# Blank products around the spreading of the first norm's weights and behind the first transposes, in a two-layer encoder trunk

## The reference

```python
def rmsnorm(x, g):
    xf = x.astype(jnp.float32)
    y = xf * lax.rsqrt(jnp.mean(xf * xf, axis=-1, keepdims=True) + EPS)
    return (y * g.astype(jnp.float32)).astype(x.dtype)

for l in range(DEPTH):                    # DEPTH = 2
    hn = rmsnorm(h, mix_pre[l])           # l = 0: the first norm, weights mix_pre[0]
    mix = rglru_mixer(hn, ...) if l == 0 else swa_sink_attention(hn, ...)
    h = h + rmsnorm(mix, mix_post[l])
    f = swiglu(rmsnorm(h, ffn_pre[l]), ffn_w_gu[l], ffn_w_down[l])
    h = h + rmsnorm(f, ffn_post[l])
```

## Time and profile before

| | us |
|---|---|
| median of 3 runs | 1109.94 (1109.6 to 1110.15) |
| the profiled execution | 1110.47 |
| its span | 1108.7 |
| TensorE products busy | 1095.7 (99% of the span) |
| TensorE weight loads busy | 980.3 (88%) |
| VectorE busy | 782.2 (71%) |
| ScalarE busy | 557.0 (50%) |
| GpSimd busy | 14.9 (1%) |

### The profile page before, as it was taken

One profiled execution on the slowest core, in us unless ns is written; L12 is line 12 of the kernel. 1 busy time (PEld: TensorE's weight loads), 2 busy tenths in 40 slices (PEclk: granted clock), 3 DMA queues, 4 the chain that ended last, 5 costly groups with the idle time before them and its releaser, 6 DMA issues.

```text
span 1108.7 us, 17385 instructions
## 1 busy us (share of the span) xinstructions
PE 1095.7 (99%) x6901; PEld 980.3 (88%) x6901; DVE 782.2 (71%) x1117; ACT 557.0 (50%) x980; POOL 14.9 (1%) x34
## 2 busy tenths in 40 slices
PE   8999999999999999999999999999999999999998
PEld 7887787889899999988888888889899999998886
DVE  5878985788688888853357888558788888863334
ACT  5377474565355555532235576555355555542223
POOL 1000000000000000000020000000000000000000
PEclk9999999999999999999999989999999999999999
DMA  6332233234133333332242132141233333343211
GB/s 203 95 106 68 77 106 114 95 98 129 41 115 115 102 90 115 134 115 95 99 118 50 39 95 58 39 114 49 86 115 114 98 94 115 115 133 99 101 48 76
DMA packets 150961, 107.22 MB, mean 97 GB/s; under 512 B 23921, under 2 KB 140769, under 8 KB 150882
## 3 DMA queue, kind: packets, MB, share of 16 engines
q1 hardware_dynamic: 150882, 106.12, 31.8%
HBM read 104.01 MB, written 2.10 MB: 96 GB/s over the span
## 4 chain that ended last, share of the span: by engine, by line
PE 97%; ACT 1%; DVE 1%; DMA 0%; issue 0%; DVEq 0%; SPq 0%
PE ps L1787 11%; PE ps L1789 11%; PE ps L1791 11%; PE ps L1565 10%; PE ps L1566 10%; PE ps L1569 10%; PE ps L1545 9%; PE ps L1547 9%; PE ps L1546 9%; PE ps L1718 1%; PE ps L1891 1%; PE ps L1575 1%; PE ps L1918 1%; PE ps L1945 1%; PE ps L1943 1%; PE ps L1941 1%
## 5 line engine op out<-in xcount | busy, mean ns | idle before, releaser
L1005 DVE TENSOR_TENSOR w_lo<-raw,w_hi 128x1024 fp32r<-128x1024 f32 x107 | 133.1, 1247 | 166.6 <-ACT w_hi L586 166.4
L586 ACT CAST w_hi<-raw 128x1024 fp32r<-128x1024 f32 x108 | 112.6, 1046 | 168.6 <-PE ps L1569 147.5
L1787 PE MATMUL ps<-t_hi,w_hi 128*128 128x256 f32 x576 | 163.2, 283 | 0.2
L1789 PE MATMUL ps<-t_lo,w_hi 128*128 128x256 f32 x576 | 163.0, 283 | 0.0
L1791 PE MATMUL ps<-t_hi,w_lo 128*128 128x256 f32 x576 | 163.0, 283 | 0.0
L1545 PE MATMUL ps<-x_hi,w_hi 128*128 128x512 f32 (+1 forms) x424 | 154.3, 364 | 0.6 <-DVE x_lo L1035 0.6
L1546 PE MATMUL ps<-x_lo,w_hi 128*128 128x512 f32 (+1 forms) x424 | 151.6, 358 | 0.0
L1547 PE MATMUL ps<-x_hi,w_lo 128*128 128x512 f32 (+1 forms) x424 | 151.5, 357 | 0.0
L1565 PE MATMUL ps<-w_hi,t_hi 128*128 128x512 f32 x352 | 137.2, 390 | 0.0
L1566 PE MATMUL ps<-w_lo,t_hi 128*128 128x512 f32 x352 | 137.0, 389 | 0.0
L1791 PE MATMUL ps<-x_hi,w_lo 128*128 128x256 f32 x432 | 122.3, 283 | 0.0
(11 more groups left out here) (218 smaller groups left out, 2160.4 us busy)
## 6 DMA issues: line engine op xcount, KB each, us to landing
raw<-in_ffn_w_gu SPq DMA_DIRECT2D x88, 512.0 KB, 4.4
raw<-in_ffn_w_down SPq DMA_DIRECT2D x44, 512.0 KB, 3.3
raw<-in_a_w_in SPq DMA_DIRECT2D x24, 512.0 KB, 3.9
raw<-in_a_w_out SPq DMA_DIRECT2D x12, 512.0 KB, 3.3
raw<-in_b_w_q SPq DMA_DIRECT2D x16, 256.0 KB, 3.3
raw<-in_b_w_o SPq DMA_DIRECT2D x16, 256.0 KB, 3.8
h<-in_x SPq DMA_DIRECT2D x4, 512.0 KB, 5.5
result<-h SPq DMA_DIRECT2D x3, 512.0 KB, 2.6
```

What stands on the lines that cost most here:

```text
L586: nc.scalar.copy(halves(t)[0], raw[:, t % 4, :]).then_inc(w_hi_ready, 1)
L1005: v.tensor_tensor(lo, raw[:, t % 4, :], hi.bitcast(F32), ALU.subtract).then_inc(w_lo_ready, 1)
L1787: nc.tensor.matmul(ps[:, b, 0:HS], w_hi[:, slot, cols], hi, start=start, stop=False, skip_group_check=True)
L1789: nc.tensor.matmul(ps[:, b, 0:HS], w_hi[:, slot, cols], lo, start=False, stop=False, skip_group_check=True)
```

## The change

- A tile `blank` of 128 x 512 in bf16 is laid where `y_hi` will be later. VectorE fills it with zeros as its first instruction and counts `blank_ready`.
- TensorE first waits for it and then runs three products of 128 x 128 with 128 x 512 of it into bank 5, whose result is not used (`busy`). Then it waits for the identity and the norm weights as before.
- The spreading is cut into four pieces of 256 columns, with a blank product behind each. `gain_spread` is counted once for each half, and VectorE waits for the first half before its first part and for the second before its second.
- A blank product follows each of the first four groups of four transposes.
- TensorE takes `first_half(1)` ahead of `first_turn(4)`. ScalarE casts tile 1 ahead of the square of block 2, and tile 2 ahead of the high part of block 2. VectorE takes the low part of tile 1 ahead of the normalising of block 2, and that of tile 2 ahead of the low part of block 2.

```diff
--- before.py
+++ after.py
@@ -195,6 +195,7 @@
     dist_i = sb("dist_i", [P, WIN], I32, at["e_u"] + 4 * P)
     dist_n = sb("dist_n", [P, WIN], F32, at["e_u"] + 8 * P)
     gain_row = sb("gain_row", [1, D], F32, at["y_lo"])
+    blank = sb("blank", [P, S], BF16, at["y_hi"])
 
 
     at["top"] = U
@@ -307,6 +308,7 @@
         xhi_ready = sem("xhi_ready")
         xlo_ready = sem("xlo_ready")
         eps_ready = sem("eps_ready")
+        blank_ready = sem("blank_ready")
         xf_ready = sem("xf_ready")
         t_ready = sem("t_ready")
         thi_ready = sem("thi_ready")
@@ -616,11 +618,11 @@
             split_hi(0)
             for i in range(4):
                 first_high(i)
+            split_hi(1)
             square_x(2)
-            split_hi(1)
             square_x(3)
+            split_hi(2)
             first_high(4)
-            split_hi(2)
             first_high(5)
             act.wait_ge(lam_abs, 1)
             nc.scalar.activation(sp_t[:, 1, :], sp_t[:, 0, :], ACT.Exp, scale=-1.0).then_inc(lam_exp, 1)
@@ -1020,8 +1022,8 @@
                 t, k0, k1 = START_PARTS[i]
                 n = pre_at(-1, t)
                 r = reciprocal(n) if k0 == 0 else rstd[:, n:n + 1]
-                if i == 0:
-                    dve.wait_ge(gain_spread, 1)
+                if i < 2:
+                    dve.wait_ge(gain_spread, i + 1)
                 if t >= 2:
                     dve.wait_ge(first_turned, 2 * t - 2)
                 cols = slice(k0 * P, k1 * P)
@@ -1035,15 +1037,16 @@
                 v.tensor_tensor(x_lo[:, k0:k1, tok], turned_in(t)[:, k0:k1, :], x_hi[:, k0:k1, tok].bitcast(F32),
                                 ALU.subtract).then_inc(first_lo, 1)
 
+            v.memset(blank[:, :], 0.0).then_inc(blank_ready, 1)
             for i in range(4):
                 normalise_x(i)
             for i in range(4):
                 first_low(i)
+            split_lo(1)
             normalise_x(4)
-            split_lo(1)
             normalise_x(5)
+            split_lo(2)
             first_low(4)
-            split_lo(2)
             first_low(5)
 
 
@@ -1658,12 +1661,23 @@
                     token_half(b, 2, t, 1)
 
 
+            def busy(n):
+
+                for _ in range(n):
+                    nc.tensor.matmul(bank(5), blank[:, 0:P], blank[:, :], start=True, stop=True)
+
+            pe.wait_ge(blank_ready, 1)
+            busy(3)
             pe.wait_ge(ident_ready, 1)
             pe.wait_ge(gain_landed, 16)
             for half in range(2):
-                ins = nc.tensor.matmul(bank(6 + half), ones_row[:, :], gain_row[:, half * S:half * S + S], start=True,
-                                       stop=True)
-            ins.then_inc(gain_spread, 1)
+                for part in range(2):
+                    cols = slice(half * S + part * HS, half * S + part * HS + HS)
+                    ins = nc.tensor.matmul(ps[:, 6 + half, part * HS:part * HS + HS], ones_row[:, :], gain_row[:, cols],
+                                           start=True, stop=True, skip_group_check=True)
+                    if part == 1:
+                        ins.then_inc(gain_spread, 1)
+                    busy(1)
 
             def first_turn(i):
                 t, k0, k1 = START_PARTS[i]
@@ -1680,9 +1694,10 @@
 
             for i in range(4):
                 first_turn(i)
+                busy(1)
             first_half(0)
+            first_half(1)
             first_turn(4)
-            first_half(1)
             first_turn(5)
             first_half(2)
             pe.wait_ge(params_landed, 16 * 8)
```

## The result

| | before | changed |
|---|---|---|
| median of 20 runs | 1109.73 (1106.67 to 1111.52) | 1110.53 (1109.83 to 1113.47) |
| profiled execution, its span | 1110.47, 1108.7 | 1110.2, 1108.4 |

The ratio of the two is 1.0017, 95% interval 1.001 to 1.0024: the changed kernel is slower by 1.1 to 2.7 us. The forecast was 2.6 us less. The profiled execution of before was one of its long ones, so the two traces have nearly the same span although the kernels differ.

What follows compares the result with a forecast made beforehand. TensorE, busy 99%, was taken as the bound. 2.3 us from the pace, 0.2 from the start and 0.1 from the switch made 2.6 less than 1109.94: 1107.3 us, range 1105.4 to 1111.0.

Steps and rivals of the forecast that it cites:

- if the one-row passes count with the blanks: Start of TensorE's queue: one-row spreading passes and blanks together raise the clock, so transposes and first tile run fast; 2.3 us.
- The rise: Doubling of TensorE's pace, forecast at 5.5 to 6.4 us, after unbroken work from 1.15; in the earlier trace at 16.9.
- Before 11.70 to 16.95: First tile's 24 projection products, taken as slow before; forecast 11.5 to 14.4, gain with the start 2.55 us.
- the slower rival: TensorE's start: blanks don't raise the clock, first product at 12.7, 1.0 late; time 1110.4, chance 0.17.
- Blank, piece, blank: Spreading: 256-column pieces cost the same 3.4 us in all, a blank 0.43 slow; second normalising waits about 0.1 us.
- The one of the late rise: TensorE's start: pace doubles only during transposes, at 12.8, first product near 12.6; gain 1.3, time 1108.6, chance 0.13.
- The later fall of the clock: Attention part, 634.72 to 644.96: a rival said this slow stretch goes away, worth 4.7 us; time 1102.6, chance 0.12.
- the memset: VectorE's filling of the blank tile at the start: ready between 0.8 and 1.4, taken as 1.1, cost nothing.
- the spreading's start: TensorE after the three first blanks: spreading begins some 0.2 us late (0 to 0.6) against 2.23.
- the fast tile once the clock is up: First tile: 24 products 0.12 us apart, 2.9 us instead of 5.25.
- the order without a hole: Tile 1 right behind tile 0: no TensorE wait appears, though two places have only 0.15 to 0.75 us of room.
- the gain from one switch less: Transposes of block 2 moved next to block 3's save one switch between the two kinds, about 0.1 us.

Runs made afterwards that it cites:

- e11: e1 with the spreading done three times over, 10.57 us of one-row passes; one profiled execution, not timed, rise at 21.64.
- e12: Changed kernel with the spreading's pieces multiplying 128 rows (ones by zeros with the weights in the first row); one profiled execution, 1112.9 us.
- e4: As e3, but the spreading multiplies 128 rows, zeros except the weights in the first; ratio to before 1.0000 (0.9991 to 1.0008).
- e1: Kernel before with only the new order of the engines' steps, no blanks, spreading uncut; ratio to before 0.9999 (0.9991 to 1.0007).
- e2: Changed kernel with every blank product left out, spreading still in four pieces, new order kept; ratio to before 1.0004 (0.9994 to 1.0014).
- e3: Changed kernel with the spreading uncut, one-row, and three blanks behind it; ratio to before 0.9998 (0.9988 to 1.0008).
- e5: Changed kernel with blanks only where TensorE idles: three behind the uncut spreading, one behind the fourth transpose group; ratio to before 0.9992 (0.9983 to 1.0002).
- e6: Changed kernel without the four blanks behind the transposes; ratio to before 1.0019 (1.0008 to 1.0031).
- e7: Changed kernel once more, no edit; ten executions, ratio to before 1.0017 (1.0008 to 1.0027), shortest span 1107.8.
- e8: Kernel before once more, no edit; one profiled execution, span 1106.6.
- e9: Kernel before with 15 tiny one-row products behind the spreading and the blank tile's memset; ratio to before 1.0006 (0.9994 to 1.0018).
- e10: e5 repeated to narrow its interval; ratio to before 0.9990 (0.9981 to 0.9998).

## Why the prediction was wrong

**The step that failed: "if the one-row passes count with the blanks".** It was marked as the assumption of the forecast, and it carried 2.3 of the 2.6 us. The rise was forecast for 5.5 to 6.4 and came at 12.02 and 13.86. e11 refutes the assumption alone; e12 (9.49) and e4 (8.10) show the early rise with 128 rows in its place, though with a spreading that starts 1.5 us later. Only one row and 128 were tried, nothing between. What the clock did follow in all fourteen traces is full-array work: the rise came 3.2 to 5.4 us after the start of an unbroken stretch of it, in the changed kernel 3.2 and 5.1 us after the start of the spreading's last blank. (Start and rise: before 11.70, 16.90; changed 8.79, 12.02; e1 7.45, 10.78; e2 12.47, 16.53; e3 6.29, 11.46; e4 4.12, 8.10; e5 6.04, 9.99; e6 8.78, 13.29; e7 8.78, 13.86; e8 7.35, 11.38; e9 7.37, 11.65; e10 6.16, 10.27; e11 18.11, 21.64; e12 4.12, 9.49.) Not every stretch brought it: the transposes of 3.7 us in before's first trace, e2 and e11 did not. The row that could have warned me was in the earlier trace rows and I used it only for a rival: 3.75 us of one-row passes had left the pace slow.

**The baseline.** "Before 11.70 to 16.95" was one of two starts. I gave the moment of the rise a spread of 0.35 us in the gain and weighed two values, 5.2 and 4.4. e8 and e1 show that the sixteen transposes can bring it at 10.8 to 11.4, so that the first tile has no slow stretch at all; by the spans that is the case in something under half of the executions. So even a perfect change at this place could win some 1 us in the mean (an estimate: 2.1 in 34 of 58 executions), not 2.3. The three runs within 0.55 us, which I took as a sign of one start, were a small sample: over 20 runs the kernel spreads over 4.9 us. From one execution to the next the rise shifts with the same start (11.38 in e8, 16.90 in the first trace), and I had let that change only the spread. In the slower rival I had put the transposes beside the one-row passes, as work that left the pace slow in the first trace. But they can bring the rise: in e1 transposes are the only work between 7.45 and 11.0, the rise is at 10.78, and the products behind them start 0.12 apart from the second on. They do not always do it: before's first trace has the rise at 16.90, 5.8 us behind their end at 11.06, and e11 at 21.64, 4.2 us behind theirs at 17.47.

**The cost of interleaving.** Blank, piece, blank was priced by its columns: 0.43 + 0.85. It measured 1.69, a stall of 0.41 four times. The start 0.35 late, four blanks (1.7) and four stalls (1.6) are 3.7 us more on TensorE; the time between the spreading's last column (2.23 + 3.41 = 5.64 before) and 7.39 took 1.75 of them, and the first transposes came 1.8 late, at 9.19 instead of the 7.4 to 7.6 of either case. With the 0.5 of the blanks behind the transposes (e6) that is the 2.3 us of the late first product.

**The rivals.** The one of the late rise named what the pace did: it put the rise at 12.8, in the transposes, and the traces have 12.02 and 13.86. It failed on the start, with the transposes at 7.6 and the first product at 12.6 where they are at 9.19 and 13.98, and so on the sign. The slower rival had the right sign and nearly the time (1110.4 against 1110.53) by the wrong sum, which is luck. It put the first product at 12.7 and left the rise at 16.9. In fact the product is at 14.0 and the rise at 12 to 14. Both errors cancel. And two terms of the result were in no case of mine: the wait at 587 costs 1.0 to 1.2 us, and in both traces of the changed kernel the attention part gives 1.4 to 1.5 back. Both traces have a span 1.8 us above e8's, and these terms add up to it: 2.0 + 1.2 - 1.4 and 2.3 + 1.0 - 1.5.

**The later fall of the clock** moved, as its rival said it might (6.83 us in one trace, none in the attention part of e7), but 4.7 us was far too much for it. Count from the transposes behind the first layer (L1575 or L1578, 583.80 in e8, 587.15 in e7) to the end of the span. That is 522.8 us in before and e8, with the fall of 10.24 us; 521.3 in e7 without that fall; 521.4 in the changed kernel's first trace (fall from 636.66); but 524.1 in e5 and 524.0 in e12, where a fall of the same 6.83 us comes at 648.28 and 651.20. So the whole fall is worth 1.5 us, and where it comes is worth up to 2.7. In e7, where the record has full speed up to 1106.13, TensorE waits for VectorE instead:

```profile
643.80 1.34 PE L1933 MATMUL ps<-ident,s_sb 64*128 64x64 f32 x11 [0.99 <-DVE s_sb L1469]
...
649.02 0.30 PE L1956 MATMUL ps<-p_hi,v_hi 128*128 128x128 f32 x1 [1.61 <-DVE p_lo L1476]
```

Its longest such waits were 1.07 and 0.60 before; two of 0.99 and 1.61 appear, and in the sum over the rounds 2.8 us of waits come back (p_lo 2.9 and s_sb 1.6 us in e7, 1.1 and 0.6 before). 4.7 less 2.8 leaves 1.9, near the 1.5 counted; before's executions with a mean clock of 0.999 begin at a span of 1104.9 where those at 0.994 begin at 1106.5. I had priced the slow stretch by TensorE alone. e5 and e12 have both costs: the same two long waits (0.99 and 1.62 in e5), and then the fall.

**What was right**: the memset (0.27, at 0.86), the spreading's start (2.58, 0.35 late), the fast tile once the clock is up (13.98 to 16.9), the order without a hole, the gain from one switch less, and that a shift at the start reaches the end.

**What stays open.** Three of the changed kernel's 20 spans are 1111.2 to 1111.7 and one of its next ten is 1111.3; no trace shows one of them. A later fall placed as in e5 would give 1108.4 + 2.7 = 1111.1 (an estimate), and their mean clock of 0.996 is e5's, but that is not shown. How large a share of the 1.9 us the 16 KB load has is known from traces (waits of 1.14 and 0.95 in the changed kernel's, 0.84 in e9), not from a timed comparison that could tell it apart. What decides where the clock falls in the attention part is open.

## What to carry to other kernels

Don't count one-row products as work that raises TensorE's clock (10.57 us of them without a rise in e11); 128-row ones did raise it here, mostly zeros as they were (at 8.10 in e4, at 9.49 in e12). Such filler was free only where the engine would be idle (e5: first product at 11.67, before 11.70); ahead of or between steps that others wait for, it was paid for in full (first product at 13.98), with a stall at each change between one-row passes and 128-row ones (0.30 and 0.10 us). Before forecasting a gain from the clock, look at several executions: a single trace may show the unlucky one of two starts, and the other has the gain already (16.90 and 11.38 here). Where an engine's slow stretch is priced, ask which other engine's wait it was hiding (2.8 us of VectorE's here). And before naming the cause of a time, compare the traces behind the edited part as well: here a wait at 587 us and a moved fall of the clock at 640 us were each as large as the effect under study.

## What the runs showed of the hardware

- At a granted clock of 0.50 the products of 512 columns start 0.43 us apart (641.59, 642.02 in before), 1.2 columns a nanosecond, the pace of the slow tile as well (256 in 0.213). At 1.00 they start 0.227 apart and those of 256 columns 0.120 (medians of before's trace), so that 256 columns more take 0.107, 2.4 a nanosecond. These two paces are what the forecast calls 1.2 and 2.4 GHz; the traces give shares of the clock, not hertz.
- Ten microseconds of unbroken one-row float32 passes left the pace slow (0.85 us a pass, the products behind them 0.21 apart until 21.66, e11); with 128 rows of mostly zeros in their place the rise came 4.0 and 5.4 us after their start (e4, e12).
- Sixteen float32 transposes alone on the engine for 3.6 us can bring the rise (10.78 in e1) or not (16.90 in before's first trace, 16.53 in e2, 21.64 in e11).
- Between a one-row float32 pass and the bf16 blank behind it lie 0.30 us more than the columns take, and 0.10 on the way back (changed kernel: piece at 2.58, blank at 3.73, piece at 4.26); with 128 rows there is neither (1.28 for two passes of 256 and a blank of 512, e12).
- With fifteen products more on TensorE at the start, a load of 16 KB from the instruction queue, at 575 to 580 us, comes about 4 us earlier (5.0 us after a weight tile's issue in e8, 1.1 in e9). GpSimd then waits longer for that tile (6.26 us in e9, 4.95 in e8) and TensorE waits 0.84 to 1.14 us behind VectorE's addition.
- One and the same fall of the clock to 0.50 for 6.83 us made the rest of the kernel 1.4 us shorter than before's fall of 10.24 us, or 1.3 us longer, by where it came (636.66; 648.28).
- VectorE's addition of two 128 x 1024 tiles takes 1.23 us alone (before, 582.08) and 2.14 (e9) to 2.44 (changed kernel) beside GpSimd's multiplication of the same size. In all five traces that have it (changed kernel, e6, e7, e9, e12), it ends 1.08 us after GpSimd's does, whichever of its own starts.
